# Triangular inverse of an RWKV-7 recurrence: block-diagonal products as two 64x64 tiles in place of one 128x128

## What is computed

```python
def step(S, inp):
    r_t, w_t, k_t, v_t, a_t, b_t = inp
    sa = jnp.einsum('bhvk,bhk->bhv', S, a_t)
    S = S * w_t[:, :, None, :] + sa[..., None] * b_t[:, :, None, :] + v_t[..., None] * k_t[:, :, None, :]
    return S, jnp.einsum('bhvk,bhk->bhv', S, r_t)
```

## Time and profile before

| What | us |
|---|---|
| Median of the runs shown | 4627.36 |
| The three runs | 4637.39, 4627.36, 4625.19 |
| Span of the profiled execution | 4629.5 |
| TensorE busy in it | 4104.1 (89%) |
| VectorE busy | 1701.1 (37%) |
| ScalarE busy | 1208.8 (26%) |
| GpSimd busy | 451.8 (10%) |

### The profile page before, as it was taken

One profiled execution on the slowest core, in us unless ns is written; L12 is line 12 of the kernel. 1 busy time (PEld: TensorE's weight loads), 2 busy tenths in 40 slices (PEclk: granted clock), 3 DMA queues, 4 the chain that ended last, 5 costly groups with the idle time before them and its releaser, 6 DMA issues. The chain is left out here.

```text
span 4629.5 us, 73073 instructions
## 1 busy us (share of the span) xinstructions
PE 4104.1 (89%) x26980; PEld 3677.6 (79%) x26980; DVE 1701.1 (37%) x2304; ACT 1208.8 (26%) x1815; POOL 451.8 (10%) x614
## 2 busy tenths in 40 slices
PE   6999886888778899899989999778887788989997
PEld 6999883448666799899989989634676667989997
DVE  4333433115444443433343333421354443443333
ACT  2222222222222222222232222322222223222222
POOL 0000022001333000000000000410033330000000
PEclk9999997889888899999999999879888878999999
DMA  2222223421000122222222222144210002222222
GB/s 77 77 87 78 70 72 95 145 73 55 7 8 6 39 81 82 68 79 84 69 78 80 83 77 73 48 131 145 64 30 6 6 6 62 82 77 76 83 79 64
DMA packets 510260, 312.98 MB, mean 68 GB/s; under 512 B 31810, under 2 KB 472812, under 8 KB 509906
## 3 DMA queue, kind: packets, MB, share of 16 engines
q1 hardware_dynamic: 501198, 308.75, 22.2%
q10 hardware_dynamic: 8964, 3.05, 0.3%
HBM read 302.10 MB, written 9.64 MB: 67 GB/s over the span
## 5 line engine op out<-in xcount | busy, mean ns | idle before, releaser
L291 PE MATMUL dense<-h_hi,whi 128*128 128x288 f32 x4800 | 1434.2, 299 | 87.0 <-DVE h_lo L377 54.8
L292 PE MATMUL dense<-h_lo,whi 128*128 128x288 f32 x4800 | 1423.4, 297 | 0.0
L293 PE MATMUL dense<-h_hi,wlo 128*128 128x288 f32 x4800 | 1418.0, 295 | 0.0
L275 DVE TENSOR_TENSOR wlo<-raw,whi 128x1024 fp32r<-128x1024 f32 x492 | 602.3, 1225 | 1657.6 <-ACT whi L271 1657.4
L291 PEld LDWEIGHTS dense<-h_hi,whi 128*128 128x128 f32 x4800 | 906.3, 189 | 97.4 <-issue 80.4
L271 ACT ACTIVATE whi<-raw 128x1024 fp32r<-128x1024 f32 x492 | 521.6, 1061 | 1724.3 <-PE dense L293 1685.9
L293 PEld LDWEIGHTS dense<-h_hi,wlo 128*128 128x128 f32 x4800 | 911.2, 190 | 0.0
L292 PEld LDWEIGHTS dense<-h_lo,whi 128*128 128x128 f32 x4800 | 908.7, 189 | 0.0
L291 PE MATMUL dense<-ffn_a_hi,whi 128*128 128x288 f32 x1408 | 416.8, 296 | 0.0
L292 PE MATMUL dense<-ffn_a_lo,whi 128*128 128x288 f32 x1408 | 415.4, 295 | 0.0
L293 PE MATMUL dense<-ffn_a_hi,wlo 128*128 128x288 f32 x1408 | 413.9, 294 | 0.0
(11 more groups left out here) (338 smaller groups left out, 4970.2 us busy)
## 6 DMA issues: line engine op xcount, KB each, us to landing
raw<-in_w_in_dram SPq DMA_DIRECT2D x124, 512.0 KB, 3.8
raw<-in_ffn_w_gate_dram SPq DMA_DIRECT2D x88, 512.0 KB, 3.9
raw<-in_ffn_w_up_dram SPq DMA_DIRECT2D x88, 512.0 KB, 3.8
page<-in_cache_k_dram SPq DMA_DIRECT2D x128, 256.0 KB, 3.4
page<-in_cache_v_dram SPq DMA_DIRECT2D x128, 256.0 KB, 4.3
raw<-in_ffn_w_down_dram SPq DMA_DIRECT2D x64, 384.0 KB, 3.1
raw<-in_ffn_w_down_dram SPq DMA_DIRECT2D x64, 320.0 KB, 2.9
raw<-in_w_out_dram SPq DMA_DIRECT2D x16, 512.0 KB, 3.6
```

What stands on the lines that cost most here:

```text
L275: dve.tensor_tensor(self.wlo[s][:], self.raw[s][:], self.whi[s][:].bitcast(F32), ALU.subtract)\
L291: pe.matmul(o, w_hi, hi[:, c, t], start=(first and c == 0), stop=False)
L292: pe.matmul(o, w_hi, lo[:, c, t], start=False, stop=False)
L293: mm = pe.matmul(o, w_lo, hi[:, c, t], start=False, stop=(last and c == chunks - 1))
```

## The change

On TensorE, each product at lines 1395 and 1401 is issued as two, one per head: rows 0 to 63 of the stationary and the moving matrix with columns 0 to 63, written to partitions 0 to 63, and rows 64 to 127 with columns 64 to 127, written to partitions 64 to 127 of the same PSUM bank. The blocks off the diagonal are no longer written by these products; they hold what the transposes of the same bank have written, which is zero. The transposes, the copies, the additions and the masks stay whole. The signal stays on the last matmul of a group. TensorE's loop over the pairs of heads becomes a loop written out, so that its waits compare with constants; the other engines keep theirs.

```diff
-                with pe.Fori(0, CB) as p:
+                for p in range(CB):
                     Qt.loop(p)
...
+                    head_rows = (slice(0, 64), slice(64, P))
+
                     def turn(j, g):
...
                             for i in range(GW):
-                                mm = pe.matmul(inv_bank(g)[:, i * P:(i + 1) * P], Lm[:, g * GW + i, :], T[:, g * GW + i, :],
-                                               start=True, stop=True)
+                                for r in head_rows:
+                                    mm = pe.matmul(inv_bank(g)[r, i * P + r.start:i * P + r.stop], Lm[r, g * GW + i, r],
+                                                   T[r, g * GW + i, r], start=True, stop=True)
                             Qt.did(mm, f"w{j}_{g}")
...
                             for i in range(GW):
-                                mm = pe.matmul(inv_bank(g)[:, i * P:(i + 1) * P], W1[:, g * GW + i, :], TT[:, g * GW + i, :],
-                                               start=True, stop=True)
+                                for r in head_rows:
+                                    mm = pe.matmul(inv_bank(g)[r, i * P + r.start:i * P + r.stop], W1[r, g * GW + i, r],
+                                                   TT[r, g * GW + i, r], start=True, stop=True)
                             Qt.did(mm, f"dt{j}_{g}")
```

## The result

The changed kernel takes 4646.76 us in the median of 10 runs (4636.1 to 4657.27); the kernel before, on the same chip, 4626.27 (4622.29 to 4643.39, 10 runs). The ratio is 1.0041, with an interval of 1.0028 to 1.0053. That is slower by 20 us, where 4604 was forecast, and just outside the range (4644). The profiled execution has a span of 4647.5 us, 18.0 above that of before.

The account below looks back on a forecast made before the run. TensorE's issue was taken to set the inversion's level. Eight pairs saving 26.6 us, less 3.3 for changing shape, left 23.3 off 4627.4: 4604 us, with an 8-in-10 range of 4597 to 4644.

Parts of the forecast that it names:

- The small record: Inversion products: two heads' quarter records run side by side, 6 x 0.058 = 0.35 us a group against 0.667.
- rival B: Inversion groups: the two heads run one after the other, TensorE stays the bound; about 4641 us, chance 0.28.
- Where the level goes: Steady inversion level: the bound moves from TensorE to VectorE; new level 4.66 us, 0.68 less.
- the change of shape: Inversion levels: switching from whole to quarter products costs 0.08 us in each of 40 levels, 3.3 us.
- First level and sum: Inversion: first level 0.60 us less, four others 0.68 each; 3.32 us a pair, 26.6 over eight pairs.
- the bound of A: Inversion: the main case, quarters overlap; 4596 to 4614 us, low end including half-clock first levels; chance 0.50.
- The loop written out: TensorE's loop over pairs: at most 0.5 us gained at turns, no stop for instructions; taken as nothing.
- Clock: Steady levels and scan: granted clock is 1.00 and was left there, with no time added.
- Rival D: Inversion: the clock falls to half, a level costs 5.98 us, 26 us more in all; 4653 us, chance 0.05.
- The handover: Inversion to scan: first product starts 0.13 us after the last addition, so a microsecond saved shortens the span equally.

## Why the prediction was wrong, step by step

**The small record, and rival B: right.** Taken at the lower end, 0.35 us a group between first starts. Measured: a group of twelve in 0.55 us against the 0.51 reckoned (5 x 0.058 + 0.222), heads overlapping. The Trainium skill, "TensorEngine Tiling (Array Packing)", Gotcha 1: PSUM Pressure, states that different row tiles cannot access the same PSUM bank simultaneously, which spoke for rival B. The trace disagrees: both heads write one bank, in different partitions, and their records start 0.007 us apart.

**Where the level goes: right.** VectorE bounds it. Forecast 4.66, measured 4.74; VectorE idle for 1.23, forecast 1.12. The difference is the 0.08 that was set aside for the change of shape: the weight loads show 0.17 us of "issue" ahead of the first tile of a level, and nothing on the way back. With a whole record's tail waited out, 0.164 in place of 0.08, it would have been 4.82. The Trainium skill, same page, Key Properties, states that a change of mode drains the engine. The trace doesn't contradict it, but the price is half of what the prediction reckoned by it. From the changed kernel's timeline:

```profile
1178.29 0.78 PEld L1398 LDWEIGHTS extra<-rwkv_over_T,rwkv_over_Lm 64*64 64x64 f32 x24 [0.17 <-issue]
```

**First level and sum: right in kind, too small.** The inversion fell from 31.4 to 27.3 us in the mean of the pairs, 4.07 each, where 3.32 - 0.41 = 2.9 was forecast. By the starts of the levels, 1.90 came from the three steady levels in the middle (three times 5.34, against 4.64 and twice 4.74), 0.21 from the last level, where the scan's first product now follows the last addition after 0.26 us instead of 0.13, and 1.94 from the first. The first was the miss: the earlier trace rows showed a level of a pair that starts at the full clock. Six of the eight pairs of before start theirs with 3.4 us at half clock, and their first level takes 9.4 to 9.6 us and not 7.5. The changed kernel has those 3.4 us in all eight pairs, and takes 7.0 to 7.25 all the same, since TensorE has slack there. What the last level gave was 0.21, and not 0.68. In the bound of A stood "more gain in the first levels of pairs that start at the half clock", as a margin and not as a term.

**The loop written out: priced as code, which costs nothing; its real cost was missed.** "I take nothing" looked at instructions and at the turn of a pair. The levels indeed stayed (5.30 against 5.34). But the stop ahead of the scan grew from 0.81 to 0.94 us. The loop by itself costs 0.2 to 0.3% in the median, as its two experiments show, and filling the stop takes that away.

**Clock: the step that failed.** "In the steady levels and the scan the granted clock is 1.00 ... I leave it there." It stays there in the levels and not in the scan. Six scans took 30.7 us in place of 24.2: 39 us, less 3 that pair 7 of before had lost in the same way. Rival D had the clock fall *in* the inversion, priced from the inversion's own work, and was given 0.05. Its total, 4653, is close by chance: no steady level of an inversion fell in this kernel. D named the scan only as evidence against itself: it keeps 1.00 with 128 records in 24.00 us. The earlier trace rows showed that of one scan, pair 0's, and it was taken for all eight. In the same trace the scan of pair 7, which starts at 1.00 as well, runs at 0.75 in the mean. So the row showed that a scan can keep the clock, not that it always does, nor how late it is back once it has fallen: 27.3 us in the changed kernel. "Outside the inversion nothing may change by more than a shift of clock phases, of a few us" was the test that failed, and it pointed to the right place.

**The handover.** The earlier trace rows were read for "a microsecond saved in a level is a microsecond of the span". They also showed 0.81 us in which TensorE stands still. That it would grow was in the forecast's own terms: TensorE's last groups get shorter and VectorE's additions behind them keep their 0.56 each. What a longer stop there would set off was not asked. The faster engine arrived early at the one place where being early cost something.

**Left open.** Of the 18.0 us, 9.2 lie outside the recurrences, 7.4 of them between those of the two layers, in code that the change doesn't touch; the half-clock time there is 225 us against 192. The other profiles have 198 to 232 there, so this stretch varies by itself, and no run isolates it. The 5.6 us behind the scan are of the same kind: those stages have 13.7 us of half clock in each pair, where before they had 10.2 in six and 17.1 in two. Why six scans fell and two not, or one behind the same stop with only the last level tiled, is shown in part: the stops are alike to 0.03 us, and the six differ from the two by 0.1 to 0.3 us in how long before them the clock had last risen. That points to timing against the chip, but no run moved a scan's start and nothing else. And the longer stop and the lighter last level were told apart only in part. With whole products the stop was lengthened to 1.20 us and not to 1.40, and with half the columns scans fell at 0.94; most of these counts come from one profile each.

## What to carry to other kernels

When an edit makes TensorE faster in a dense stage, look at where it will then stand still, and at what stage comes next: a sparse one may keep the full clock and yet be slow to regain it, so a half microsecond more of waiting in front of it can cost six. Before giving up such an edit, fill the stop with a few products that nobody reads, or leave the last step unoptimised; here either turned +0.4% into -0.5%. Read the granted clock of a stage as a state carried over from the stage before, not as a property of the stage itself.

## What the runs showed of the hardware

- **Quarter tiles overlap within one bank of the result.** 64x64 products of float32 in opposite corners of the array start 0.007 us apart, 0.030 us a record on average; eight records of 64 by 64 that share all rows are 0.058 apart.
- **A narrower moving tile saves nothing under a whole stationary.** 0.111 us a record with 64 moving columns, as with 128. With 64 stationary columns and the same 64 moving ones it is 0.058.
- **A busy TensorE can stay at half clock.** With 64 moving columns under a whole stationary it had a record for 27.30 of 27.30 us in pair 0, and the granted clock was 0.50 all the while. Quarter tiles, 283 records in 17 us with gaps, kept the 1.00 that they started from.
- **A stop of about a microsecond can be followed by a halved clock for most of a stage.** Behind 1.40 us the clock stayed low for 27.3 us in the scans of six pairs; behind 0.94, in the written-out loop's second profile, for 28.7 us in two and 10.2 in one. With the stop filled to 0.09 us none fell.
- **One profile can miss it.** The same kernel gave spans of 4624.8 and 4640.6 us, with one scan slightly and three more heavily affected. When a median of many runs and a profile disagree, a second profile is worth a run.
